# Identity transposes in TensorE's waits, and the first up products ahead of the second rows, in a two-layer streaming encoder

## Chip, cores and metric

One core of one Trainium2 chip. The metric is the device time of one execution in microseconds (us), the median of three runs.

## What is computed

Two layers of an encoder over 640 rows of 1024 numbers (512 of a prompt, 8 streams of 16 frames), all in fp32. Cut to what matters here, one layer is:

```
xn = rms_norm(x, norm1)
q|k|v|q_idx|k_idx|w_idx|u|v_s|g_a|g_b = xn @ w_in
att = sparse attention of q over the keys that the indexer selects
sg  = chunked spatial gating of u and v_s
h   = x + (sigmoid(g_a) * (att @ w_pa) + sigmoid(g_b) * (sg @ w_pb)) @ w_out
xf  = rms_norm(h, norm2)
g   = the best of 4 groups for a row (softmax of xf @ w_rg + b_rg)
e   = the best two of its 8 experts (softmax of xf @ w_re + b_re), weights that sum to 1
y   = h + sum over the two of weight * ((silu(xf @ w_eg[e]) * (xf @ w_eu[e])) @ w_ed[e])
```

After the second layer stands a last `rms_norm`. The new keys, values, index keys and gating rows are outputs too.

## The kernel before

Every engine has its own program, written out by hand, and the engines wait for each other on semaphores. TensorE's program (`pe`, from line 729) runs each layer in this order. `norm_transposes` (L734) turns a tile of 128 rows into `xt`: eight transposes by the identity per tile (L749), four to a bank, with banks 0 to 3 in turn. `proj_job` (L770) multiplies a tile by a block of `w_in` (L763). Attention, gating (L1045) and the output product (L1096) follow. While the output product runs, `route` (L1062) gives each finished tile's router logits.

Then comes the **dispatch**, the stretch in which rows are assigned to experts. VectorE picks each row's experts (`tile_route`), TensorE counts their ranks by products with a triangle of ones (`ranks`, L1069 and L1070), VectorE turns ranks into one-hot matrices (`place_front`, `place_back`, `dispatch`), and TensorE multiplies these into a table of rows (`table_rows`, L1076, and the product of L1121 for the rows beyond 64 of an expert). Between these steps TensorE waits for VectorE: `chosen_ready`, `onehot_ready` (2, 3 and 4), `need_ready`. With the table, GpSimd gathers rows from DRAM into `xin` (L687).

The **expert blocks** are 17 per layer, `NB`; each holds two experts with 64 rows each. For block b, `rows_step` waits for the gather and transposes the 128 rows by the identity (L1129); VectorE's `rows_out` copies them to `xin_t` with a gain (L1806), two copies of 512 columns per block; `up_step` multiplies by the two experts' gate and up weights (L1142, 32 instructions); ScalarE takes the silu (L1394); VectorE's `hidden_rows` multiplies (L1813); `across_step` transposes the hidden rows (L1148); `down_step` multiplies by the down weights (L1153); ScalarE copies out (L1403), and GpSimd scatters the result to `yd` (L692). TensorE's order is rows 0, rows 1, up 0, and then for each b: rows b+2, across b, up b+1, down b. `rows_step(b)` with b of 2 or more also waits for the copies of all blocks before b (`xin_ready`).

VectorE's order at the start of the blocks is fixed by its own program:

```
rows_out(0, 0)
rows_out(1, 1, 4)
pair_weights(L)
for b in range(NB):
    hidden_rows(b, b % XBUF, b % 2)
    if b + 2 < NB:
        rows_out(b + 2, b % 2)
```

`pair_weights` is `gates` (from L1484) and two instructions more (L1614, L1615); its result is used after the last block.

The weights of 12 experts fit at a time, in `places`. SyncE's program issues the loads of experts 12 and on in order: the gate and up weights of a pair when the up products of the block that holds their place are done (`gu_psum`, L416), then the down weights when that block's down products are done (`y_psum`, L426), and only then the next pair. Gathers and scatters go through GpSimd's own queue.

At the **boundary of the layers**, SyncE waits for the last scatters (`y_out`) and reloads each row's two results (L542); VectorE's `combine` adds them (L1833), and TensorE's `norm_transposes` for the next layer waits for each tile's sum (`x_new`).

Of the kernel before, what the change touches and what calls it, by code (L numbers as in the profile page):

```python
# [21 lines left out]
P = 128  # L22
# [39 lines left out]
NB = PLAIN + ALWAYS // 2  # L62
# [13 lines left out]
YBUF = 2  # L76
# [30 lines left out]
def filled(i, L, e):  # L107

    here = [v for v in LOADED if v % PLACES == i]
    return L * len(here) + len([v for v in here if v <= e])  # L110
# [18 lines left out]
def prior(name, L):  # L129

    return L * PER_LAYER[name]
# [25 lines left out]
def build(nc, a, o):  # L157
    ctx = ExitStack()
    with ctx:
# [3 lines left out]
        def sem(name):  # L163
            return ctx.enter_context(nc.semaphore(name))
# [116 lines left out]
        banks = [ctx.enter_context(nc.psum_tensor(f"bank{i}", [P, BLK], F32)) for i in range(8)]  # L281
# [47 lines left out]
        y_out = [sem(f"y_out{z}") for z in range(YBUF)]  # L329
# [31 lines left out]
        def gathers(q):  # L361

            return 16 * len(range(q, NB, XBUF))

        def scatters(z):

            return 16 * len(range(z, NB, YBUF))
# [362 lines left out]
        def _(pe):  # L730
            pe.wait_ge(s_ident, 1)
            idm = ident[:, :]

            def norm_transposes(phase, tiles, L):  # L734
                for t in tiles:
                    if phase:
                        pe.wait_ge(mt_done, prior("mt_done", L) + 2 * NT)
                        pe.wait_ge(xo_done, prior("xo_done", L) + 2 * t + 2)
                    elif L:
                        pe.wait_ge(x_new, prior("x_new", L - 1) + t + 1)  # L740
                    else:
                        pe.wait_ge(s_x[t], 16)
                    for hf in range(2):
                        n = 2 * t + hf
                        if n >= 4:
                            pe.wait_ge(xt_done, prior("xt_done", L) + 2 * NT * phase + n - 3)
                        for k in range(4):

                            mm = pe.transpose(banks[n % 4][:, k * P:(k + 1) * P],  # L749
                                              x[:, t, 4 * hf + k:D:KD], idm)  # L750
                        mm.then_inc(xt_psum, 1)

            for L in range(DEPTH):
# [16 lines left out]
                def proj_job(n):  # L770
                    u, t = PROJ_JOBS[n]
                    if t == 0:
                        wait_unit(u)
                    if u == KU:
                        if t + 1 < NT and (t or L):
                            norm_transposes(0, (t + 1,), L)
                        pe.wait_ge(xt_done, prior("xt_done", L) + 2 * t + 2)
                    if n >= 4:
                        pe.wait_ge(proj_free, prior("proj_free", L) + n - 3)
                    mm = project(u, t, banks[4 + n % 4][:, 0:width(u)], width(u))  # L780
                    mm.then_inc(proj_psum, 1)
                    if u == KU and t == 0 and not L:
                        norm_transposes(0, (1,), L)
                    if t == NT - 1 and u != IU:
                        pe.drain().then_inc(unit_done, 1)

                def fill(n):
# [10 lines left out]
                    if k1 == KD:  # L798
                        mm.then_inc(proj_psum, 1)
                        if t == NT - 1:  # L800
                            pe.drain().then_inc(unit_done, 1)

                norm_transposes(0, (0,), L)
                for n in range(2 * NT):
                    proj_job(n)

# [259 lines left out]
                def ranks(a, b):  # L1066
                    pe.wait_ge(chosen_ready, prior("chosen_ready", L) + b)
                    out = banks[RANK_BANK[a]][:, 0:EXPERTS * (b - a)]
                    pe.matmul(out, before, scr[:, P + EXPERTS * a:P + EXPERTS * b], start=True, stop=False)  # L1069
                    pe.matmul(out, ones, scr[:, P + EXPERTS * (NT + a):P + EXPERTS * (NT + b)],  # L1070
                              start=False, stop=True).then_inc(count_psum, 1)

                def table_rows(tiles):
                    for m in range(2 * tiles[0], 2 * tiles[-1] + 2):
                        for h in range(2):
                            mm = pe.matmul(banks[7][BR * h:BR * h + BR, 0:EXPERTS // 2], rank_hot[:, m, :],  # L1076
                                           place_hot[:, m, h:EXPERTS:2], start=(m == 0), stop=(m == 2 * NT - 1))
                    return mm

                for n in range(2 * NT):  # L1080
# [20 lines left out]
                    if t >= 1 and c == 0:  # L1101
# [4 lines left out]
                pe.wait_ge(onehot_ready, prior("onehot_ready", L) + 2)  # L1106
                pe.wait_ge(xo_done, prior("xo_done", L) + 2 * NT)
                table_rows(range(4))
                ranks(4, 5)

                pe.matmul(banks[6][0:EXPERTS, 0:1], earlier_tiles[:, NT - 1, :], ones[:, 0:1], start=True, stop=False)
                pe.matmul(banks[6][0:EXPERTS, 0:1], chosen[:, NT - 1, :], ones[:, 0:1], start=False, stop=True).then_inc(count_psum, 1)
                pe.wait_ge(onehot_ready, prior("onehot_ready", L) + 3)
                table_rows([4]).then_inc(table_psum, 1)
                pe.wait_ge(need_ready, prior("need_ready", L) + 1)
                pe.matmul(banks[6][:, P:P + EXPERTS + 1], need_rows, before[0:EXPERTS, 0:EXPERTS + 1],
                          start=True, stop=True).then_inc(start_psum, 1)
                pe.wait_ge(onehot_ready, prior("onehot_ready", L) + 4)
                for m in range(2 * NT):
                    for h in range(2):  # L1120
                        mm = pe.matmul(banks[7][BR * h:BR * h + BR, 256:256 + n_over // 2], rank_hot[:, m, :],  # L1121
                                       over_hots[:, m, h:n_over:2], start=(m == 0), stop=(m == 2 * NT - 1))
                mm.then_inc(table_psum, 1)
                pe.wait_ge(table_ready, prior("table_ready", L) + 1)

                def rows_in(b, q, first=0):

                    for k in range(KD):
                        mm = pe.transpose(banks[first + k // 4][:, (k % 4) * P:(k % 4 + 1) * P], xin[q][:, k:D:KD], idm)  # L1129
                    mm.then_inc(xin_psum[L], 1)  # L1130

                def up(two, z):
                    for k in range(KD):
                        for h in range(2):
                            if two[h] is places[SPLIT]:
                                for m in range(2):
                                    mm = pe.matmul(banks[2 + z][BR * h:BR * h + BR, P * m:P * m + P],
                                                   xin_t[z][:, k, BR * h:BR * h + BR], two[h][0][m][:, P * k:P * k + P],
                                                   start=(k == 0 and m == 0), stop=(k == KD - 1 and m == 1))
                                continue  # L1140
                            w = two[h][0].rearrange("p (m k f) -> p m k f", m=2, k=KD)
                            mm = pe.matmul(banks[2 + z][BR * h:BR * h + BR, 0:2 * P].rearrange("p (m f) -> p m f", m=2),  # L1142
                                           xin_t[z][:, k, BR * h:BR * h + BR], w[:, :, k, :],
                                           start=(k == 0), stop=(k == KD - 1))
                    mm.then_inc(gu_psum[L], 1)
# [12 lines left out]
                def two_of(b):  # L1158
                    return [places[(2 * b + h) % PLACES] for h in range(2)]

                def rows_step(b):
                    pe.wait_ge(x_in[b % XBUF], gathers(b % XBUF) * L + (16 * (b // XBUF) + 16))
                    if b >= 2:
                        pe.wait_ge(xin_ready[L], 2 * b)
                    rows_in(b, b % XBUF, 4 if b == 1 else 0)

                def up_step(b):
                    for h in range(2):
                        e = 2 * b + h
                        if b != OVER_AT:  # L1170
                            pe.wait_ge(up_in[e % PLACES], 32 * filled(e % PLACES, L, e))
                        else:
                            pe.wait_ge(more_up, 32 * ALWAYS * (L + 1))
                    pe.wait_ge(xin_ready[L], 2 * b + 2)
                    if b >= 2:
                        pe.wait_ge(h_done[L], b - 1)
                    up(two_of(b), b % 2)
# [17 lines left out]
                    down(two_of(b), b % 2)  # L1195

                rows_step(0)
                rows_step(1)
                up_step(0)
                for b in range(NB):  # L1200
                    if b + 2 < NB:
                        rows_step(b + 2)
# [696 lines left out]
```

## Time and profile before

| | |
|---|---|
| runs | 1440.35 us median of three, 1437.21 to 1441.36 |
| profiled execution | 1441.81 us, span 1440.0 us |
| TensorE matmul busy | 1315.8 us, 91% of the span, 5724 instructions |
| TensorE weight loads | 723.0 us, 50% |
| VectorE, ScalarE, GpSimd busy | 533.0 us, 339.7 us, 220.7 us |
| mean granted TensorE clock | 0.957 of full speed |
| HBM read, written | 199.44 MB, 27.78 MB |

Busy time is an average over stages with different limits. A granted clock of 1.00 is 2.4 GHz and one of 0.50 is 1.2 GHz; a stretch with both shows a number between. In the chain of waits, a row gives the time at which a piece of the chain starts, its length, and what it is: work of an engine at a line, a transfer, or "issue" where the profile shows nothing that was waited for. Some matmul records can be missing from a trace.

### The profile page before, as it was taken

To read this page: it belongs to the slowest core of one execution; us is meant where nothing else is said; L and a number is where in the kernel's file an instruction comes from. 1 tells how busy PE (TensorE), PEld (TensorE's weight loads), DVE (VectorE), ACT (ScalarE), POOL (GpSimd) and SP (SyncE) were. 2 spreads that over 40 slices of the span, in tenths; PEclk is the share of its full clock that TensorE was granted. 3 is DMA by queue.
4 is the path that set the end of the run, shared out by engine and by line. 5 is a ranking of instruction groups with operands and counts; after the bars stand their busy time and mean duration, and the time that the engine had idled before them with its cause. 6 is when DMAs were issued, how large, how long until landed. Compare 5 with 4: busy or idle time off the path is not lost.

```text
span 1440.0 us, 15437 instructions
## 1 busy us (share of the span) xinstructions
PE 1315.8 (91%) x5724; PEld 723.0 (50%) x5724; DVE 533.0 (37%) x1542; ACT 339.7 (24%) x773; POOL 220.7 (15%) x304
## 2 busy tenths in 40 slices
PE   7999999999999998998699999999999999979880
PEld 5654446544444555565385544464444445555550
DVE  1278895201110236321244779731011013462215
ACT  2132467200000101221213325651000010012221
POOL 6011024000000001233240200600000000022413
PEclk9989999999999997999799999999999999979995
DMA  8302102502402413999681111052060060379986
GB/s 241 117 13 60 59 1 72 175 0 66 153 0 95 183 73 134 372 409 402 260 207 59 51 33 49 8 145 95 0 219 0 0 263 30 117 273 404 405 314 242
DMA packets 96061, 208.77 MB, mean 145 GB/s; under 512 B 26529, under 2 KB 35969, under 8 KB 95985
## 3 DMA queue, kind: packets, MB, share of 16 engines
q1 hardware_dynamic: 81376, 181.27, 35.5%
q0 software_dynamic: 14608, 26.49, 5.3%
q8 instruction: 47, 0.77, 0.2%
q14 instruction: 30, 0.24, 0.0%
HBM read 199.44 MB, written 27.78 MB: 158 GB/s over the span
## 4 chain that ended last, share of the span: by engine, by line
PE 80%; DMA 5%; ACT 4%; issue 3%; DVE 3%; PEld 2%; PEldq 1%; SPq 0%; POOL 0%; POOLq 0%; ACTq 0%; DVEq 0%
PE bank L763 35%; PE bank L1045 10%; PE bank L1096 10%; PE bank L1142 7%; PE bank L796 3%; PE bank L1153 3%; DMA uv<-xd,mb 2%; PE bank L1129 2%; PE bank L845 1%; DMA more<-in_w_eu 1%; PE bank L1062 1%; PE bank L749 1%; PE bank L949 1%; PE bank L849 1%; PEldq L988 1%
## 5 line engine op out<-in xcount | busy, mean ns | idle before, releaser
L763 PE MATMUL bank<-ring,xt 128*128 128x512 f32 (+1 forms) x1120 | 433.9, 544 | 7.8 <-DMA ring<-in_w_in 5.0
L763 PEld LDWEIGHTS bank<-ring,xt 128*128 128x128 f32 x1120 | 213.8, 193 | 209.8 <-issue 190.2
L1766 DVE TENSOR_TENSOR scr<-scr,bank 128x512 f32<-128x512 f32 x20 | 13.7, 687 | 368.6 <-PE bank L1045 368.6
L1096 PE MATMUL bank<-ring,xt 128*128 128x512 f32 x320 | 141.3, 594 | 0.0
L557 POOL TENSOR_SCALAR stat<-stat 128x1 f32<-128x1 f32 (+1 forms) x27 | 10.4, 387 | 797.7 <-ACT uv L1229 614.1
L1373 ACT ACTIVATE scr<-bank,stat 128x512 f32<-128x512 f32 x40 | 25.3, 684 | 347.8 <-PE bank L763 347.8
L1096 PEld LDWEIGHTS bank<-ring,xt 128*128 128x128 f32 x320 | 59.3, 190 | 67.0 <-issue 67.0
L796 PE MATMUL bank<-ring,xt 128*128 128x512 f32 x160 | 76.7, 614 | 0.0
L1045 PE MATMUL bank<-ring,att 128*128 128x512 f32 x160 | 72.5, 596 | 2.2 <-ACT sgt L1365 1.8
L1045 PE MATMUL bank<-ring,sgt 128*128 128x512 f32 x160 | 71.9, 592 | 0.0
L763 PE MATMUL bank<-more,xt 128*128 128x512 f32 x160 | 70.3, 592 | 0.0
L1806 DVE TENSOR_TENSOR xt<-bank,gain 128x512 f32<-128x512 f32 x68 | 43.8, 685 | 66.4 <-PE bank L1129 66.4
L1142 PE MATMUL bank<-ring,xt 128*64 128x256 f32 x480 | 66.1, 382 | 1.5 <-issue 1.5
L1477 DVE MAX8 stat<-mb 128x8 f32<-128x256 f32 (+3 forms) x114 | 61.7, 541 | 3.0
L1477 DVE MATCH_REPLACE8 mb<-stat,mb 128x256 f32<-128x256 f32 (+3 forms) x114 | 59.7, 524 | 0.0
L692 POOL DMA_INDIRECT yd<-scr,mb x34 | 34.1, 1002 | 154.9 <-ACT scr L1403 149.7
L1813 DVE SCALAR_TENSOR_TENSOR xt<-bank,uv,xt 128x128 f32<-128x128 f32 x34 | 11.9, 351 | 116.5 <-ACT xt L1394 116.5
L1142 PE MATMUL bank<-qkv,xt 128*64 128x256 f32 x192 | 50.7, 424 | 3.2 <-issue 3.2
L1129 PEld LDWEIGHTS bank<-ident,uv 128*128 128x128 f32 x272 | 35.5, 197 | 31.9 <-issue 20.7
L1045 PEld LDWEIGHTS bank<-ring,att 128*128 128x128 f32 x160 | 29.9, 190 | 41.4 <-issue 39.1
L1142 PEld LDWEIGHTS bank<-ring,xt 128*64 128x64 f32 x480 | 39.2, 137 | 22.2 <-issue 4.3
L1777 DVE TENSOR_TENSOR x<-x,bank 128x512 f32<-128x512 f32 x20 | 13.8, 688 | 97.6 <-PE bank L1096 97.6
(288 smaller groups left out, 1806.1 us busy)
## 6 DMA issues: line engine op xcount, KB each, us to landing
ring<-in_w_in SPq DMA_DIRECT2D x12, 2048.0 KB, 9.4
ring<-in_w_ed SPq DMA_DIRECT2D x32, 512.0 KB, 17.8
ring<-in_w_eg SPq DMA_DIRECT2D x26, 512.0 KB, 11.1
ring<-in_w_eu SPq DMA_DIRECT2D x26, 512.0 KB, 17.5
ring<-in_w_out SPq DMA_DIRECT2D x4, 2048.0 KB, 12.9
qkv<-in_w_eg SPq DMA_DIRECT2D x12, 512.0 KB, 7.8
qkv<-in_w_eu SPq DMA_DIRECT2D x12, 512.0 KB, 10.1
more<-in_w_ed SPq DMA_DIRECT2D x12, 512.0 KB, 8.8
```

The lines of the kernel that those rows point to most:

```text
L692: pool.indirect_dma_start(out=yd, in_=yout[z], in_offset=None, out_offset=bass.IndirectOffsetOnAxis(ap=index(b, 1, q), axis=0), bounds_che ...
L749: mm = pe.transpose(banks[n % 4][:, k * P:(k + 1) * P], x[:, t, 4 * hf + k:D:KD], idm)
L763: mm = pe.matmul(out, xt[:, k, t * P:(t + 1) * P], rhs[:, k, :], start=(k == 0), stop=(k == KD - 1))
L796: mm = pe.matmul(banks[7][:, :], xt[:, k, t * P:(t + 1) * P], rhs[:, k, :], start=(k == 0), stop=(k == KD - 1))
L1045: mm = pe.matmul(b[2 + half_][:, :], src[:, j, t * P:(t + 1) * P], w[:, 4 * half_ + j, :], start=(j == 0), stop=(j == 3))
L1096: mm = pe.matmul(banks[5 + n % 3][:, :], xt[:, k, t * P:(t + 1) * P], w[:, k, :], start=(k == 0), stop=(k == KD - 1))
L1129: mm = pe.transpose(banks[first + k // 4][:, (k % 4) * P:(k % 4 + 1) * P], xin[q][:, k:D:KD], idm)
L1142: mm = pe.matmul(banks[2 + z][BR * h:BR * h + BR, 0:2 * P].rearrange("p (m f) -> p m f", m=2), xin_t[z][:, k, BR * h:BR * h + BR], w[:, :, ...
L1153: mm = pe.matmul(banks[4 + c][BR * h:BR * h + BR, :], hidden_t[z][:, BR * h:BR * h + BR], two[h][1][c] if two[h] is places[SPLIT] else two ...
L1373: ins = act.activation(scr[:, c0:c0 + 512], banks[4 * (n % 2) + m][:, :], ACT.Sigmoid, scale=rs1[:, n % NT:n % NT + 1])
L1477: make(*args, **kwargs).then_inc(dve_chain, 1)
L1806: V.tensor_tensor(xin_t[z][:, 4 * hf:4 * hf + 4, :], banks[first + hf][:, :].rearrange("p (k r) -> p k r", k=4), gain[:, L, 1, 4 * hf:4 * ...
```

## The change

TensorE gets a helper, `keep_busy(n, bank)`, that transposes the identity n times into the first 128 columns of a bank. Nothing reads the results. It is called

- at the start of layer 0: 8 times ahead of the first tile's transposes and 22 times behind them, bank 3;
- at the start of layer 1: 22 times ahead of the first tile's transposes, bank 3, behind a new wait for the last scatter of layer 0 (`y_out` of the last block's buffer);
- in each layer's dispatch, bank 1: 3 times ahead of `ranks(4, 5)`, 6 ahead of the last tile's `table_rows`, 9 ahead of the products of L1121, and 3 ahead of the wait for the table.

And `up_step(0)` now stands ahead of `rows_step(1)`. The other engines' programs are as before. The diff:

```diff
@@ -731,6 +731,11 @@
             pe.wait_ge(s_ident, 1)
             idm = ident[:, :]
 
+            def keep_busy(n, bank):
+
+                for _ in range(n):
+                    pe.transpose(banks[bank][:, 0:P], idm, idm)
+
             def norm_transposes(phase, tiles, L):
@@ -800,7 +805,12 @@
+                if L:
+                    pe.wait_ge(y_out[(NB - 1) % YBUF], scatters((NB - 1) % YBUF) * L)
+                keep_busy(22 if L else 8, 3)
                 norm_transposes(0, (0,), L)
+                if L == 0:
+                    keep_busy(22, 3)
                 for n in range(2 * NT):
                     proj_job(n)
@@ -1106,21 +1116,25 @@
                 table_rows(range(4))
+                keep_busy(3, 1)
                 ranks(4, 5)
 
                 pe.matmul(banks[6][0:EXPERTS, 0:1], earlier_tiles[:, NT - 1, :], ones[:, 0:1], start=True, stop=False)
                 pe.matmul(banks[6][0:EXPERTS, 0:1], chosen[:, NT - 1, :], ones[:, 0:1], start=False, stop=True).then_inc(count_psum, 1)
+                keep_busy(6, 1)
                 pe.wait_ge(onehot_ready, prior("onehot_ready", L) + 3)
                 table_rows([4]).then_inc(table_psum, 1)
                 pe.wait_ge(need_ready, prior("need_ready", L) + 1)
                 pe.matmul(banks[6][:, P:P + EXPERTS + 1], need_rows, before[0:EXPERTS, 0:EXPERTS + 1],
                           start=True, stop=True).then_inc(start_psum, 1)
+                keep_busy(9, 1)
                 pe.wait_ge(onehot_ready, prior("onehot_ready", L) + 4)
...
                 mm.then_inc(table_psum, 1)
+                keep_busy(3, 1)
                 pe.wait_ge(table_ready, prior("table_ready", L) + 1)
@@ -1195,8 +1209,8 @@
                 rows_step(0)
+                up_step(0)
                 rows_step(1)
-                up_step(0)
                 for b in range(NB):
```

Line numbers move: the identity transposes are L737, and L749 becomes L754, L763 L768, L1069 L1079, L1076 L1086, L1121 L1134, L1129 L1143, L1142 L1156, L1148 L1162.

TensorE at the start of layer 0, first before and then after (an x stands for that many products of the program in a row):

```order
L729 UNCONDITIONAL_BRANCH
L749 MATMUL bank<-ident,x 128x128 x8
L763 MATMUL bank<-ring,xt 128x276 x8
L749 MATMUL bank<-ident,x 128x128 x16
L763 MATMUL bank<-ring,xt 128x276 x8
```

```order
L729 UNCONDITIONAL_BRANCH
L737 MATMUL bank<-ident 128x128 x8
L754 MATMUL bank<-ident,x 128x128 x8
L737 MATMUL bank<-ident 128x128 x22
L768 MATMUL bank<-ring,xt 128x276 x8
```

Thirty transposes of the identity stand around those of the first rows, ahead of the first products with weights (L768).

TensorE in the dispatch of layer 0, from the ranks of the last tile to the first up products, first before and then after (`scr` holds the counts, `uv` the one-hot matrices and the gathered rows):

```order
L1069 MATMUL bank<-scr 128x32
L1070 MATMUL bank<-scr 128x32
L1111 MATMUL bank<-scr 32x1
L1112 MATMUL bank<-scr 32x1
L1076 MATMUL bank<-uv 64x16 x4
L1116 MATMUL bank<-scr 128x33
L1121 MATMUL bank<-uv 64x10 x20
L1129 MATMUL bank<-ident,uv 128x128 x16
L1142 MATMUL bank<-more,xt 64x256
L1142 MATMUL bank<-qkv,xt 64x256
```

```order
L737 MATMUL bank<-ident 128x128 x3
L1079 MATMUL bank<-scr 128x32
...
L737 MATMUL bank<-ident 128x128 x6
L1086 MATMUL bank<-uv 64x16 x4
L1128 MATMUL bank<-scr 128x33
L737 MATMUL bank<-ident 128x128 x9
L1134 MATMUL bank<-uv 64x10 x20
L737 MATMUL bank<-ident 128x128 x3
L1143 MATMUL bank<-ident,uv 128x128 x8
L1156 MATMUL bank<-more,xt 64x256
L1156 MATMUL bank<-qkv,xt 64x256
```

Before the up products there now stand eight transposes of gathered rows, those of block 0, instead of sixteen; the sixteen of blocks 1 and 2 follow behind them:

```order
L1156 MATMUL bank<-qkv,xt 64x256
L1143 MATMUL bank<-ident,uv 128x128 x16
L1162 MATMUL bank<-ident,xt 128x128
L1156 MATMUL bank<-qkv,xt 64x256
L1156 MATMUL bank<-sgt,xt 64x256
```

The transpose of the hidden rows of block 0 (L1162), which waits for VectorE, stands behind these sixteen, and the up products of block 1 behind that.

## Rows read from the trace of the kernel before

**Rows 1.** The page's slices: 40 of 36 us each, granted clock and transfers.
```profile
PEclk9989999999999997999799999999999999979995
GB/s 241 117 13 60 59 1 72 175 0 66 153 0 95 183 73 134 372 409 402 260 207 59 51 33 49 8 145 95 0 219 0 0 263 30 117 273 404 405 314 242
```

**Rows 2.** Timeline of TensorE at the start: start us, us, instruction [idle before, ended by].
```profile
4.51 1.95 PE L749 MATMUL bank<-ident,x 128*128 128x128 f32 x8 [4.51 <-DMA x<-in_x_prompt]
11.43 5.65 PE L763 MATMUL bank<-ring,xt 128*128 128x276 f32 x16 [4.97 <-DMA ring<-in_w_in]
...
18.90 3.99 PE L763 MATMUL bank<-ring,xt 128*128 128x276 f32 x16
```

**Rows 3.** Stretches around L1056: busy PE, PEld, DVE, ACT, POOL, then clock, transfers.
```profile
469.00:472.20 3.20, 1.02 (x10) 0.99 (x10) 2.58 (x10) 0.29 (x1) 0.00 (x0) 1.00 1.07 347
472.20:475.60 3.40, 3.40 (x18) 3.40 (x17) 0.00 (x0) 2.59 (x5) 0.00 (x0) 0.50 0.96 377
475.60:478.00 2.40, 2.40 (x19) 2.09 (x18) 0.00 (x0) 2.27 (x5) 0.00 (x0) 0.99 1.02 408
```

**Rows 4.** Timeline of TensorE in the dispatch of layer 0.
```profile
565.94 0.64 PE L1069 MATMUL bank<-scr 128*128 128x32 f32 x2 [0.92 <-DVE scr L1516]
...
569.10 0.61 PE L1076 MATMUL bank<-uv 128*64 128x16 f32 x8 [1.79 <-DVE uv L1555]
...
572.86 2.31 PE L1121 MATMUL bank<-uv 128*64 128x10 f32 x40 [2.58 <-DVE uv L1586]
575.95 1.94 PE L1129 MATMUL bank<-ident,uv 128*128 128x128 f32 x8 [0.78 <-DMA uv<-xd,mb]
```

**Rows 5.** Chain of waits, first expert blocks of layer 0: start us, us, what.
```profile
580.22 4.25 PE bank L1142 x32
...
586.32 0.36 DVE xt L1813
...
587.05 3.60 PE bank L1142 x32
...
593.56 3.60 PE bank L1142 x32
```

**Rows 6.** Timeline of VectorE around the pair weights of layer 0.
```profile
577.93 1.29 DVE L1806 TENSOR_TENSOR xt<-bank,gain 128x512 f32<-128x512 f32 x2 [0.75 <-PE bank L1129]
...
581.46 0.17 DVE L1484 TENSOR_REDUCE mb<-mb 128x5 f32<-128x20 f32 x1
...
583.94 0.49 DVE L1615 TENSOR_REDUCE mb<-scr 128x10 f32<-128x320 f32 x1
```

**Rows 7.** Timeline of SyncE's queue, loads of weights in layer 0.
```profile
585.81 0.45 SPq L416 DMA_DIRECT2D qkv<-in_w_eu  x1
592.41 0.33 SPq L426 DMA_DIRECT2D more<-in_w_ed  x1
```

**Rows 8.** Issue to landing, us: loads issued at 585.81, at 592.41, at 1286.21.
```profile
qkv<-in_w_eu SPq DMA_DIRECT2D x1, 512.0 KB, 9.8
more<-in_w_ed SPq DMA_DIRECT2D x1, 512.0 KB, 4.5
qkv<-in_w_eu SPq DMA_DIRECT2D x1, 512.0 KB, 10.5
```

**Rows 9.** Chain of waits, late expert blocks of layer 0 and the boundary.
```profile
641.67 18.68 DMA more<-in_w_eu
...
663.11 5.36 PE bank L1142 x32
...
704.23 3.17 DMA yd<-scr,mb
```

**Rows 10.** Timeline of TensorE at the boundary of the layers.
```profile
713.70 1.97 PE L749 MATMUL bank<-ident,x 128*128 128x128 f32 x8 [11.44 <-DVE x L1833]
716.94 1.94 PE L749 MATMUL bank<-ident,x 128*128 128x128 f32 x8 [1.27 <-DVE x L1833]
718.67 5.23 PE L763 MATMUL bank<-ring,xt 128*128 128x276 f32 x16
```

## The prediction

> **What bounds the kernel now.** I read the page first, its clock row and its transfer row [rows 1]; then TensorE's timeline at the places that the change touches [rows 2, 4, 10]; then the chain of waits through the first expert blocks [rows 5] and through the end of a layer [rows 9]. In [rows 1] the reader is to see two things. Each of the 40 digits of the clock row is a slice of 36 us: it stands at 9 nearly everywhere, and falls to 7 in the slice with the dispatch of layer 0 (the 16th), with the boundary of the layers (the 20th) and with the dispatch of layer 1 (the 36th). So the low clock is a matter of a few places, and the engine is near full clock otherwise. And in the slices of layer 0's expert blocks (the 17th to 19th) the transfers stand at 372 to 409 GB/s, about the highest of the run: there the weights arrive at the rate that the queue gives, and the chain waits for them, as in the 18.68 us of one load that ends it at 660.35 [rows 9]. What TensorE wins or loses in the first expert blocks must therefore get past the transfers before it reaches the end of the kernel.
>
> **The start: -1.7.** Eight transposes of the first rows took 1.95 us, 0.244 each, and the first eight products behind them 5.65 us; the next eight products took 3.99 [rows 2]. Only the clock differs between the two, so 5.65 - 3.99 = 1.66 us is what the low clock costs here. The change puts 8 transposes ahead of the first rows (8 x 0.244 = 1.95 us, before rows arrive at 4.51) and 22 behind them, from 6.46 on. At 0.244 they would end at 6.46 + 5.4 = 11.8, 0.4 us behind the weights that land for 11.43; at the price of the next paragraph's row (3.40 us for 18, 0.19 each) at 10.6, ahead of them. The ends are a loss of 0.4 and a gain of 1.66. I take the gain, since the nearest row shows such a run of transposes lifting the clock: in [rows 3] the engine did nothing but transposes from 472.2 to 475.6 at a granted clock of 0.50 (1.2 GHz), and the next stretch, transposes again, stands at 0.99 (2.4 GHz). What follows the start is TensorE's own work, so the gain stays.
>
> The Trainium skill states the contrary (TensorE: Matmul & The Clock Gate, Part 4: PE-mode transpose): the full clock does not engage for transposes, which do not count as activity of the engine in the same way. By that rule the sum would lose this gain and be 1.7 higher; by the row it keeps it. The rule comes back as a rival.
>
> **The boundary of the layers: -0.3.** The new wait ends when the last scatter has landed, 704.23 + 3.17 = 707.40 [rows 9]; the reloads behind it wait for the same event, so the wait itself costs nothing. 22 transposes then run to 711.6 (at 0.19) or 712.8 (at 0.244). The first rows' transposes start at 713.70, so nothing is delayed. But then the engine waits again: from 715.67 to 716.94 for the second rows [rows 10]. The upper end is the whole price of the low clock there: 1.94 - 1.05 for the second rows' transposes, where 1.05 is 8 at the 0.13 of [rows 3] (19 in 2.40 us), and 5.23 - 3.99 = 1.24 for the first products, together 2.1. The lower end is 0. I take -0.3, near the lower end, since between 469.0 and 472.2 a stretch with 1.02 us of transposes was enough for the clock to be at 0.50 behind it [rows 3], and from the end of the 22 until 716.94 there would be no more than one group of eight, which took 1.97.
>
> **The dispatch: 0.** Per layer 3 + 6 + 9 + 3 transposes go into four waits that TensorE has there anyway. At 0.244 they take 0.73, 1.46, 2.20 and 0.73 us, and the waits are 0.92, 1.79, 2.58 and 0.78 [rows 4]. All fit, the last by 0.05, so the cover is what VectorE and the gather do meanwhile; without it they would cost 5.1 us a layer. Do they lift the clock? Longest without a break are 9, half of what lies in the stretch of [rows 3] that lifted it, and between them stand products that are 10 or 16 columns wide. I take no gain; the upper end goes into the rival below.
>
> **The first up products ahead of the second rows: +1.5 and +0.7.** This is the part with a new wait, and what is queued behind it decides. Before, the second rows' transposes ended at 580.22 and the up products of block 0 followed [rows 5]. The copies for block 0 were done at 577.93 + 1.29 = 579.22 [rows 6], so they can now start at 579.25, 1.0 us earlier. But VectorE's order is unchanged: copy of block 0, copy of block 1, pair weights, then the hidden rows of block 0. The copy of block 1 waits for transposes that now stand behind the up products, and the pair weights, 581.46 to 583.94 + 0.49 = 584.43 or 2.97 us [rows 6], which ran beneath the up products, are now late behind it. From the end of the first up products to the second there were 2.6 us (584.47 to 587.05), with 0.73 from the hidden rows on (586.32 to 587.05) [rows 5]. Now there are 1.1 (eight transposes at 0.13) + 1.29 (copy) + 2.97 (pair weights) + 0.73 = 6.1, or 3.5 more.
>
> How much later the second up products start, S, has these ends. If the clock is full from 579.25 on, the first up takes the 3.60 of the second [rows 5], ends at 582.85, and S = 582.85 + 6.1 - 587.05 = 1.9. If it is low throughout, it takes twice that, 7.2, and S is 5.5. TensorE now idles from 577.89 to 579.25, where it used to transpose, so I expect the first up to run at the low clock for longer than before and to end at 584.5 to 585, which makes S about 3.8; and a hole of 6 us with 17 transposes in it is like the waits ahead of the up of 5.36 us at 663.11 [rows 9], which costs another 1.2 to 1.8. I take **S = 5**.
>
> What comes of S at the end? The next loads are issued behind block 0's down products, at 592.41 [rows 7], and would be issued at 597.4. The load before them was issued at 585.81 and landed 9.8 us later, at 595.6 [rows 7, 8]; the first of the next landed at 592.41 + 4.5 = 596.9, 1.3 us behind it. So the queue held 3.2 us of work at 592.41, and how much of this a later issue may use before the queue runs dry lies between 0 and 3.2; I take the middle, 1.6, which leaves a hole of 5 - 1.6 = 3.4 us. Against this, the gathers and scatters come later too: 128 rows of 1032 and of 1024 numbers, 1.05 MB, per block of 6.5 us (587.05 to 593.56 [rows 5]), at some 400 GB/s 2.6 us in 6.5, so 0.4 x 5 = 2.0 us less stands in the queue ahead of the late weights. The chain meets the transfers again at 663.11 with 3.4 - 2.0 = +1.4, say +1.5. In layer 1 the load in that place took 10.5 instead of 9.8 us [rows 8], so it has 0.7 more stock: +0.7.
>
> **The sum.** -1.7 - 0.3 + 0 + 1.5 + 0.7 = +0.2. The profiled execution took 1441.81 us; the sum makes it 1442.0. It is 1.5 above the median of 1440.35, and the runs shown spread by 4 us; against the median the forecast is 1440.35 + 0.2, **1440.5**. About 0.3%, 4.3 us, is what a measurement of this kernel can tell from no change.
>
> **The rivals.** *Slower: the queue runs dry.* The loads behind the first down products come S late and nothing makes it good: the full 5 us in each layer, less the 2.0 of the other parts, is +8.0, **1448.4**. It decides from an issue later than 592.41 + 3.2, which S = 5 exceeds. For it: the load at 592.41 landed close behind its forerunner. Against it: gathers and scatters come later by as much, and the chain waits 18.68 us for one load anyway [rows 9]. Chance 0.16.
>
> *Faster: the clock stays up.* The dispatch's transposes lift it before the first up products, and the boundary's hold it. Then S is 1.9, within the queue's 3.2, so the transfers lose nothing and have 0.4 x 1.9 = 0.8 less ahead of them in layer 0: -1.7 - 2.1 - 0.8 = -4.6, **1435.8**. For it: the run of transposes in [rows 3]. Against it: the waits between them. Chance 0.15.
>
> *Transposes do not hold the clock.* Then the added ones are idle time by another name: start and boundary give 0, the reordering stays, +2.2, **1442.6**. The trace speaks against it [rows 3]: 0.06. This is the rule of the Trainium skill's page (TensorE: Matmul & The Clock Gate, Part 4); the trace does not agree, with 0.99 behind 0.50 through transposes alone.
>
> **How the numbers follow.** The forecast has 0.63, the others 0.16, 0.15 and 0.06. The forecast's own bounds: S from 1.9 to 7, and a stock from 0 to 3.2, move each layer by some -0.8 to +4, the boundary -2.1 to 0; mostly that is 1436 to 1445. Taking in most of both rivals, I give 1435.0 to 1446.5. Faster by over 0.3% (under 1436.0): most of the second rival and a little of the forecast, 0.17. Slower (over 1444.7): the first rival and the forecast's upper edge, 0.20. Within: 0.63.
>
> **What would show it.** Right: the first eight products at 3.7 to 4.0 us instead of 5.65; the clock at 0.50 for most of the dispatch still; VectorE's pair weights behind the copy of block 1, and the second up products 4 to 6 us later against the first gather's landing; the loads behind the first down products as much later; the chain through a load at the late blocks again. Wrong: the first products still above 5 us (transposes do not count); the pair weights ahead of the copy of block 1; the clock full by the first up products; late blocks that wait 5 us longer than before in both layers.

## The result, and the profile after

The changed kernel takes **1454.31 us** (median of 6 runs, 1450.78 to 1456.42); the kernel before, beside it, 1440.86 (6 runs). The ratio is 1.0089, 95% interval 1.0068 to 1.0110: 13.4 us slower. The forecast was 1440.5, the range 1435.0 to 1446.5: wrong, and on the slow side. The profiled execution took 1453.69 us, its span 1451.9. In two of the experiments below one execution was a slow one (5552.48 us with the start's transposes alone, 1780.82 with two experts' weights early); it counts in the median given there and not in the ratio.

The page's slices, which answer to [rows 1]; a slice is now 36.3 us:

```profile
PEclk9989999999999997999899999999999999969995
GB/s 240 115 13 59 58 1 75 171 0 100 118 0 154 125 84 166 323 410 402 257 196 59 50 46 35 8 169 69 0 217 0 0 260 44 125 241 398 407 315 240
```

The clock digits hardly differ. Among the slices with dense transfers the first of the expert blocks of layer 0 stands out, the 17th: 323 GB/s, where [rows 1] had 372. There the time is looked for first.

TensorE's timeline at the start, which answers to [rows 2]:

```profile
4.69 1.97 PE L754 MATMUL bank<-ident,x 128*128 128x128 f32 x8 [1.02 <-DMA x<-in_x_prompt]
6.46 4.35 PE L737 MATMUL bank<-ident 128*128 128x128 f32 x22
11.62 3.99 PE L768 MATMUL bank<-ring,xt 128*128 128x276 f32 x16 [0.80 <-DMA ring<-in_w_in]
```

The first products take 3.99 us instead of 5.65; their weights landed 0.2 later. The start gains 1.5 us (the next group of products starts at 17.42 instead of 18.90), close to the forecast.

The chain of waits through the first expert blocks of layer 0, which answers to [rows 5]; L1156 are the up products (L1142 before), L1143 the transposes of gathered rows, L1820 the copies, L1827 the hidden rows:

```profile
574.73 1.96 PE bank L1143 x8
576.72 1.30 DVE xt L1820 x2
578.15 6.32 PE bank L1156 x32
584.47 1.10 PE bank L1143 x8
585.60 1.29 DVE xt L1820 x2
...
589.28 0.50 DVE mb L1629
589.80 0.36 DVE xt L1827
590.21 0.35 PE bank L1162
590.57 5.21 PE bank L1156 x32
595.78 1.75 PE bank L1167 x8
```

Three things are longer than in [rows 5]. The first up products take 6.32 us instead of 4.25. Between them and the second stand 590.57 - 584.47 = 6.10 us instead of 2.6: the copy of block 1 and all of the pair weights, the last of which ends at 589.28 + 0.50. And the second up products take 5.21 instead of 3.60. From the first rows' transposes to the first down products it is 595.78 - 574.73 = 21.05 us instead of 14.70 (575.95 [rows 4] to 587.05 + 3.60 [rows 5]): 6.35 us more.

SyncE's queue shows what hangs on that, and answers to [rows 7]: the last load behind the first up products, and the first behind the first down products.

```profile
586.57 0.43 SPq L416 DMA_DIRECT2D qkv<-in_w_eu  x1
597.54 0.33 SPq L426 DMA_DIRECT2D more<-in_w_ed  x1
```

It was 592.41; it is 597.54, though this execution came to the blocks 1.2 us earlier. The transfers from 586 to 606 us, 40 slices of 0.5 us, first before and then after:

```profile
GB/s 410 418 459 361 410 410 418 442 418 410 410 411 436 394 328 385 311 393 418 369 369 279 279 279 303 328 410 401 434 418 410 411 419 419 402 426 418 418 401 426
```

```profile
GB/s 401 410 410 369 393 369 377 385 393 418 418 426 254 157 198 141 0 0 0 0 0 0 0 0 0 213 295 434 393 401 328 221 270 287 295 377 369 360 401 418
```

Before, the rate never falls below 279. After, the queue is empty from 594 to 598.5, with thin slices on both sides. The dip before, from 596.5 to 598, is no sign of an empty queue: six loads had been issued from 592.41 to 595.59, and the last of them landed 10.4 us later, at 606.0; after the change a dip stands about as far behind the same loads, 221 to 295 from 601.5 to 603.5. From 592 to 604 the 24 slices have a mean of 376 GB/s before and 178 after: 2.4 MB less in 12 us, which at 410 GB/s is 5.8 us of transfers. The late end of layer 0 in the chain answers to [rows 9]:

```profile
668.10 5.36 PE bank L1156 x32
...
678.38 5.36 PE bank L1156 x32
...
709.40 3.17 DMA yd<-scr,mb
```

The up products that started at 663.11 start at 668.10, the last scatter at 709.40 instead of 704.23: 5.2 us later, 6.4 with the 1.2 us counted by which this execution came to the blocks earlier. Layer 1 repeats it; rows of the chain, first before and then after:

```profile
1276.15 3.65 PE bank L1129 x16
...
1286.70 3.60 PE bank L1142 x32
...
1406.58 3.24 DMA yd<-scr,mb
```

```profile
1281.53 1.96 PE bank L1143 x8
...
1284.94 6.21 PE bank L1156 x32
...
1297.36 5.09 PE bank L1156 x32
...
1418.55 3.24 DMA yd<-scr,mb
```

From the first rows' transposes to the first down products, 1302.45 - 1281.53 = 20.92 us instead of 1290.30 - 1276.15 = 14.15, or 6.77 more; the last scatter 11.97 later, of which 6.8 are new. So each layer ends as much later as its first down products come: from their start to the last scatter it is 113.58 us before (590.65 to 704.23) and 113.62 after (595.78 to 709.40) in layer 0, 116.28 and 116.10 in layer 1. The theory to test is therefore the first rival, **the queue runs dry**: the new order makes the first down products late, the loads behind them come late, and no part of that is made good. Against it stands a second theory, that the added transposes carry a part.

### The profile page after: what moved, and what is told of

Its sections match the earlier page's. It is cut to its first block, busy times and chain, and to the rows that moved or that the text cites. A ratio compares the mean times of both kernels' runs of the same rounds, so it can differ in the third digit from the quotient of the medians.

```text
span 1451.9 us, 15624 instructions
## 1 busy us (share of the span) xinstructions
PE 1341.3 (92%) x5818; PEld 743.2 (51%) x5818; DVE 533.1 (37%) x1542; ACT 339.5 (23%) x773; POOL 219.9 (15%) x304
## 4 chain that ended last, share of the span: by engine, by line
PE 80%; DMA 5%; ACT 4%; DVE 4%; issue 4%; PEld 2%; PEldq 1%; POOL 1%; SPq 0%; POOLq 0%; ACTq 0%; DVEq 0%
PE bank L768 34%; PE bank L1055 10%; PE bank L1106 10%; PE bank L1156 7%; DMA uv<-xd,mb 3%; PE bank L801 3%; PE bank L1167 3%; PE bank L1143 2%; PE bank L855 1%; PE bank L1072 1%; PE bank L754 1%; PE bank L959 1%; DVE x L1847 1%; PE bank L859 1%; PEldq L998 1%
## 5 line engine op out<-in xcount | busy, mean ns | idle before, releaser
L768 PE MATMUL bank<-ring,xt 128*128 128x512 f32 (+1 forms) x1120 | 432.8, 543 | 3.6 <-issue 1.8
L768 PEld LDWEIGHTS bank<-ring,xt 128*128 128x128 f32 x1120 | 213.0, 193 | 205.2 <-issue 190.4
L557 POOL TENSOR_SCALAR stat<-stat 128x1 f32<-128x1 f32 (+1 forms) x27 | 10.5, 389 | 798.7 <-ACT uv L1243 614.1
L1820 DVE TENSOR_TENSOR xt<-bank,gain 128x512 f32<-128x512 f32 x68 | 43.8, 686 | 80.9 <-PE bank L1143 80.9
L768 PE MATMUL bank<-more,xt 128*128 128x512 f32 x160 | 70.3, 592 | 0.0
L1156 PE MATMUL bank<-ring,xt 128*64 128x256 f32 x480 | 66.1, 382 | 1.2 <-issue 1.2
L1156 PE MATMUL bank<-qkv,xt 128*64 128x256 f32 x192 | 57.9, 469 | 3.5 <-issue 3.5
L1827 DVE SCALAR_TENSOR_TENSOR xt<-bank,uv,xt 128x128 f32<-128x128 f32 x34 | 11.9, 351 | 115.0 <-ACT xt L1408 114.9
L1143 PEld LDWEIGHTS bank<-ident,uv 128*128 128x128 f32 x272 | 34.1, 195 | 34.3 <-issue 23.0
L1156 PEld LDWEIGHTS bank<-ring,xt 128*64 128x64 f32 x480 | 39.2, 137 | 21.9 <-issue 4.0
L1055 PEld LDWEIGHTS bank<-ring,sgt 128*128 128x128 f32 x160 | 30.4, 190 | 38.3 <-issue 38.3
```

Of the source, the lines that this page charges most:

```text
L768: mm = pe.matmul(out, xt[:, k, t * P:(t + 1) * P], rhs[:, k, :], start=(k == 0), stop=(k == KD - 1))
L1055: mm = pe.matmul(b[2 + half_][:, :], src[:, j, t * P:(t + 1) * P], w[:, 4 * half_ + j, :], start=(j == 0), stop=(j == 3))
L1820: V.tensor_tensor(xin_t[z][:, 4 * hf:4 * hf + 4, :], banks[first + hf][:, :].rearrange("p (k r) -> p k r", k=4), gain[:, L, 1, 4 * hf:4 * ...
```

## The experiments

**1. The old order, all transposes kept.**

```diff
                 rows_step(0)
-                up_step(0)
                 rows_step(1)
+                up_step(0)
```

> The changed kernel with the second rows back ahead of the first up products; all identity transposes stay. Order theory (the loss of 13.4 us is the order alone: the second up products end 6.4 us later in each layer and nothing of it is made good): 1440.9 - 1.4 of the start = 1439.5, and the second up products of layer 0 near 585.7, 1.4 ahead of before. Transposes theory (the identity transposes in the dispatch and at the boundary carry a part of the loss, by delaying TensorE or shifting the clock): over 1441, up to the 1447 that half of the loss would give.

Measured: 1439.03 us, ratio 0.9982 (0.9969 to 0.9996). As the order theory had it; the second up products of layer 0 started at 582.18, earlier than the 585.7 given, mainly because this execution came to the blocks 3.6 us earlier than the kernel before. The chain shows one thing more, the first up products of both layers:

```profile
575.97 3.63 PE bank L1156 x32
```

```profile
1279.56 3.69 PE bank L1156 x32
```

They were 4.25 and 4.32 us: in the old order the dispatch's transposes can lift the clock ahead of them. They don't always: in the four kernels of experiments 8 to 11, with the same order and transposes, the same products took 3.69 us in four of eight cases and 4.21 to 4.67 in the others. Without the transposes, in five kernels of the old order, none took less than 4.16.

**2. The new order alone, on the kernel before**, without any transposes of the identity.

> The kernel before with the first up products ahead of the second rows and no identity transposes. Order theory: 1440.9 + 2 x 6.4 = 1453.7, between 1452.5 and 1455.5, the changed kernel's time with the start's 1.4 us given back. Transposes theory: 1447 to 1450, since half of the loss or more would be gone with the transposes.

Measured: 1452.93 us, 1.0093 (1.0068 to 1.0117). The order is the whole loss; the transposes theory falls.

**3. The pair weights ahead of the copy of block 1**, on the changed kernel (VectorE's program).

```diff
                 rows_out(0, 0)
-                rows_out(1, 1, 4)
                 pair_weights(L)
+                rows_out(1, 1, 4)
```

> The changed kernel with VectorE's pair weights ahead of the copy of block 1, so that they run beneath the first up products again. Queue theory (what counts is how late the second up products end): they start 2.1 us earlier, since the rows of block 2 still wait for that copy (586.9 + 1.2 + 0.3 = 588.4 instead of 590.5), and the shorter hole may spare 1.6 us of low clock, so 2.1 to 3.7 us less in each layer: 1454.3 - 4.2 to 7.4 = 1447 to 1450. If the loss had nothing to do with that delay (the new order hurts by the gathers or scatters it moves): no change, 1454. If there were stock for part of the delay (as I had predicted, 1.6 to 3.6 us of it), the loss would fall to 2 us a layer or less: under 1444.

Measured: 1443.75 us, 1.0025 (1.0008 to 1.0043); the profiled execution took 1447.49. The chain:

```profile
575.54 6.61 PE bank L1156 x32
...
586.03 3.60 PE bank L1156 x32
```

The hole is 586.03 - 582.15 = 3.9 us instead of 6.10, and the second up products are 1.6 us shorter: 3.8 us a layer, at the upper end of what I gave. The median lies 3 us below the range, and only the upper end of its interval (1447.6) and the profiled execution meet it; why the others are faster than the trace explains stays open. By the number alone the case with stock (under 1444) would be met; runs 4 and 5 speak against it.

**4. A delay of TensorE and nothing else**, on the kernel before, ahead of the up products of block 1; **5. the same delay six blocks later** (`b == 6`).

```diff
                     across_step(b)
+                    if b == 0:
+                        keep_busy(48, 6)
                     if b + 1 < NB:
                         up_step(b + 1)
```

> The kernel before, with 48 identity transposes between the transpose of the hidden rows of block 0 and the up products of block 1, in each layer: a delay at full clock and nothing else (48 x 0.11 = 5.3 us; no other order, VectorE as before). Queue-dry theory (the loads behind the first down products come 5.3 us later and nothing is made good): 1440.9 + 10.6 = 1451.5. Absorption as I had predicted it (a stock of 1.6 us and 0.4 of the delay, so 5.3 becomes 1.6 and 0.9): 1443.4. Clock theory (what hurts in the changed kernel is the low clock, and a delay with a busy TensorE costs little): under 1444.

> The kernel before, with the same 48 identity transposes six blocks later, ahead of the up products of block 7 (there a load takes 15 to 20 us from issue to landing, against 4.5 behind the first down products). Queue theory (a delay counts where the queue has nothing left and is hidden where loads stand in it): 1440.9, no more than 1442. If every delay of TensorE in the expert blocks reaches the end: 1451.5.

Measured: 1454.53 us, 1.0087 (1.0065 to 1.0110), and 1441.39 us, 1.0003 (0.9989 to 1.0018). The chain shows the same delay in both, at full clock, first ahead of block 1, then ahead of block 7:

```profile
587.45 5.24 PE bank L737 x48
592.69 3.60 PE bank L1147 x32
```

```profile
625.13 5.24 PE bank L737 x48
630.37 3.60 PE bank L1147 x32
```

This is the pair that decides. 5.24 us a layer, with no change of order, cost 13.4 us at one place (9.4 to 15.9 by the interval; 10.5 is the delay itself) and nothing at the other. In the profiled execution of the first, layer 1's first up products also took 5.70 us instead of 4.32, which nobody asked for (5.62 in the second). In the second, the 11th down products of layer 0 come 70.5 us behind the first instead of 65.6, and the 12th 78.1 instead of 77.8: TensorE's wait for the late loads takes the delay in. Behind the first the queue runs empty; its transfers from 586 to 606 us, in 0.5 us slices:

```profile
GB/s 410 401 442 361 401 410 393 401 410 451 426 410 386 427 320 189 90 49 25 8 0 0 0 0 0 0 180 377 377 410 434 320 107 172 246 320 320 287 320 426
```

Nothing was absorbed, and my stock of 1.6 us and credit of 0.4 of the delay (1443.4) are refuted.

**6. The low clock ahead of the first up products.** In experiment 3 these still took 6.61 us. On its kernel, six transposes go into the wait for the copy of block 0:

```diff
                 rows_step(0)
+                keep_busy(6, 5)
                 up_step(0)
                 rows_step(1)
```

> The kernel with the pair weights ahead (1443.8), and six identity transposes in the 1.47 us in which TensorE waits for the copy of block 0 ahead of the first up products (6 x 0.244 = 1.46, so they delay nothing). In all reordered runs so far the first up products ran at the low clock nearly throughout (5.2 to 6.6 us), in the old order with the same transposes they took 3.6 to 4.6. If that wait is what keeps the clock low: the first up takes 3.6 to 4.2, 2 to 2.7 us less in each layer, 1443.8 - 4 to 5.4 = 1438 to 1440. If the new order has too little work ahead of the first up products in any case (eight transposes of rows instead of sixteen): 1443.8, first up still over 5 us.

Measured: 1438.67 us, 0.9981 (0.9966 to 0.9995). The timeline of TensorE ahead of the up products, without the six and with them:

```profile
575.54 0.66 PE L1156 MATMUL bank<-more,xt 128*64 128x256 f32 x1 [1.47 <-DVE xt L1820]
```

```profile
574.60 1.48 PE L737 MATMUL bank<-ident 128*128 128x128 f32 x6
576.28 0.40 PE L1156 MATMUL bank<-more,xt 128*64 128x256 f32 x1 [0.19 <-DVE xt L1821]
```

Stretches of 4 us (busy PE, PEld, DVE, ACT, POOL, clock, transfers), again without and with; then the chain with them:

```profile
570.00:574.00 4.00, 4.00 (x37) 3.33 (x35) 2.95 (x13) 0.00 (x0) 2.10 (x3) 0.50 0.77 237
574.00:578.00 4.00, 2.53 (x13) 1.65 (x14) 3.62 (x15) 0.00 (x0) 0.00 (x0) 0.50 0.87 290
578.00:582.00 4.00, 4.00 (x22) 2.28 (x18) 0.28 (x1) 0.00 (x0) 0.00 (x0) 0.56 1.01 380
```

```profile
570.00:574.00 4.00, 4.00 (x49) 3.81 (x50) 3.56 (x16) 0.00 (x0) 2.97 (x3) 0.50 0.70 185
574.00:578.00 4.00, 3.81 (x26) 3.12 (x26) 3.15 (x14) 0.00 (x0) 0.01 (x1) 0.75 0.90 284
578.00:582.00 4.00, 3.04 (x27) 2.18 (x22) 1.82 (x4) 1.65 (x2) 0.00 (x0) 1.00 1.00 374
```

```profile
576.28 3.67 PE bank L1156 x32
```

Without the six TensorE stands still for 1.47 us while VectorE copies, and the granted clock stays at 0.50 (1.2 GHz) into the up products; with them it is at 1.00 (2.4 GHz) as they begin. The wait that the new order put ahead of the up products is what kept the clock low. Between 576.28 and 577 us it is 1.00, and layer 1's first up products take 3.67 as well. With both causes gone, the new order costs nothing against the old one (1439.03).

**7. The start's transposes alone**, on the kernel before.

> The kernel before with the 8 and 22 identity transposes at the start of layer 0 alone. If the start's gain stays to the end: 1440.9 - 1.4 = 1439.5, with first products of 4.0 us instead of 5.65 at 11.4. If transfers or a wait later in layer 0 take it back: 1440.9. If the transposes delay the first products: over 1441.3.

Measured: 1440.23 us, 0.9995 (0.9982 to 1.0009). Inconclusive: a gain of 1.5 us is within the interval, and so is none. That the first products are shorter is shown, above; that it reaches the end is not shown by this run alone.

**8 to 12. Filling the queue.** If the queue sets the end of a layer, earlier loads must pay where it is dry. Two edits of SyncE's program, on the kernel of experiment 1: expert 7's weights ahead of the wait for the second gather (`x_in[1]`), into a stretch with nothing to transfer; and the next pair's gate and up weights ahead of the last pair's down weights.

```diff
-                sp.wait_ge(x_in[1], gathers(1) * L + 16)
                 expert(7, EXPERTS * L + 7)
+                sp.wait_ge(x_in[1], gathers(1) * L + 16)
...
-                for e in range(PLACES, 2 * NB, 2):
+                for e in range(PLACES, 2 * NB + 2, 2):
...
-                    for v in units:
+                    for v in [v for v in (e - 2, e - 1) if v in LOADED and v >= PLACES]:
                         sp.wait_ge(y_psum[L], (v - PLACES) // 2 + 1)
                         expert_down(v % PLACES, EXPERTS * L + 2 * BLOCK_AT[v // 2] + v % 2, down_in[v % PLACES])
```

The first edit alone, then both, then the second alone:

> The first experiment's kernel (identity transposes, old order) with the weights of expert 7 issued ahead of SyncE's wait for the second gather, into the 4 us in which nothing is transferred (568 to 572 in layer 0): 1.5 MB or 3.7 us of transfers earlier. If the amount moved sets the end and the queue never runs dry later: 1439.0 - 2 x 3.7 = 1431.6. Queue-dry theory: the stock is only used up sooner; the loads behind the first down products are issued when they were, the queue is dry for 3 us more in front of them, and the gain is 0 to 1 us a layer: 1437 to 1439. If the load slows the first two gathers: up to 1443.

> As the one before, and SyncE issues the next pair's gate and up weights (due at that block's up products) ahead of the down weights of the pair before (due at its down products, 1.7 us later): the order in which TensorE frees the places and uses them. Queue-dry theory: 2 MB come 1.7 to 2.5 us earlier at the place where the queue is dry, so 1.5 to 3 us a layer less than the one before: 1432 to 1436. If the end is not set there: as the one before, 1437 to 1439, or more where down weights come late.

> The first experiment's kernel (1439.0) with the order of SyncE's loads alone changed: the next pair's gate and up weights ahead of the down weights of the pair before. If the two edits of the run before add up without helping each other: 1428.8 + 1.4 = 1430, nearly all of the gain from this one. If they need each other (an early load 7 pays only where the queue doesn't run dry behind it): the order alone fills a hole of 1 us a layer, 1435 to 1437, and the rest came with load 7.

Measured: 1437.59 (0.9970, 0.9955 to 0.9985), **1428.83** (0.9921, 0.9892 to 0.9951) and 1431.85 us (0.9939, 0.9918 to 0.9961). The transfers from 576 to 606 us, 40 slices of 0.75 us, with the first edit and with both:

```profile
GB/s 165 268 371 371 410 382 208 44 27 153 306 388 388 366 415 421 399 231 22 71 246 404 388 388 284 257 333 350 377 421 416 421 400 377 388 339 426 415 432 400
```

```profile
GB/s 311 273 322 322 235 317 361 306 240 180 300 393 404 406 378 410 399 421 399 361 355 404 399 432 416 416 421 394 404 426 421 399 421 433 400 416 421 393 426 426
```

The early load pays little by itself, since the queue then runs dry near 582 and near 590 instead; with the loads also issued as TensorE frees their places, it stays full from 584 on. What I had not expected is the size of the second edit: 1439.0 - 1431.9 = 7.2 us, where I had put the hole at 1 us a layer. It is not a filled queue: by 78 us behind the first down products of layer 0 the kernels with and without it had moved the same, 88.10 and 88.07 MB since the start. But the 12th down products come 73.9 us behind the first instead of 77.9 (78.1 instead of 82.2 in layer 1), and the last scatter of layer 0 109.7 instead of 113.9. So the gain is made in the late blocks, where the up products wait for gate and up weights [rows 9], which now come ahead of the down weights. That is read from the two traces; no run changes the order in the late blocks alone.

Two more stood beside these: expert 9's weights early too, and both edits on the kernel before, with no transposes.

> The kernel with both edits (1428.8), and expert 9's weights ahead of SyncE's wait for the second gather too, so 1.5 MB more before the expert blocks. If the queue has work to the end of the layer with it: up to 3.7 us a layer less, 1421.4. If the queue is dry in front of the first freed places instead: 1428 to 1429. If the first gathers, which all start from, now land behind these loads: 1 to 3 us a layer more, 1431 to 1435.

> The kernel before with the two edits of the loads and no identity transposes at all. If the transposes are worth what the first experiment showed (2.4 us) and stand beside the loads: 1428.8 + 2.4 = 1431. If they are worth more here, since every us ahead of the first up products is passed on: 1433.

Measured: 1436.34 (0.9960, 0.9944 to 0.9976) and 1432.72 us (0.9945, 0.9924 to 0.9966). The first is 7.5 us worse than with expert 7 alone, more than I gave for slower gathers. Its chain shows such a gather:

```profile
564.47 6.94 DMA uv<-xd,mb
```

In the changed kernel the first gather of the layer took 4.60 us. But the profiled execution was the fastest of that kernel, 1428.90, so where the rest of the loss lies stays open. The second differs from 1428.83 by 3.9 us in the medians, with overlapping intervals: whether the transposes are worth the 2.4 us of experiment 1 there is not shown.

## Why the prediction was wrong

**The start, -1.7: right**, -1.5 in the trace. The Trainium skill (TensorE: Matmul & The Clock Gate, Part 4: PE-mode transpose) has transposes not count for the full clock; the trace disagrees here too: 22 of them in 4.35 us, 0.20 each where eight ahead took 0.246 each, and products at 3.99 behind. Experiment 6 repeats it with six more transposes. At the start itself the low clock is read from durations alone: the granted clock of the profile reads 1.00 from 0 to 20 us in both kernels. And the last stretch of [rows 3] is not transposes alone, as the prediction says: two products of L1096 stand in it from 477.31 on. That the gain reaches the blocks no run shows: executions come to layer 0's first rows at 575.95 (before), 574.73 (after) and 573.21 us (experiment 2, without the start's transposes).

**The boundary, -0.3: nothing came of it.** The 22 transposes there end in time, and the clock is up behind them: 0.97 in the first rows' transposes, which take 1.16 us instead of 1.97. But it is at 0.50 again in the 1.46 us in which TensorE waits for the sums and in the second rows' transposes, which take 1.94 us again, and the first products take 5.64, no less than the 5.23 of [rows 10]:

```profile
719.00 1.16 PE L754 MATMUL bank<-ident,x 128*128 128x128 f32 x8 [1.80 <-DVE x L1847]
721.62 1.94 PE L754 MATMUL bank<-ident,x 128*128 128x128 f32 x8 [1.46 <-DVE x L1847]
723.36 5.64 PE L768 MATMUL bank<-ring,xt 128*128 128x276 f32 x16
```

From the last scatter of layer 0 to the first rows' transposes of layer 1 it is 572.13 us after (709.40 to 1281.53) and 571.92 before (704.23 to 1276.15).

**The dispatch, 0: right in this kernel**, whose first up products ran at the low clock all the same. In the old order the same transposes shortened them to 3.63 and 3.69 us in experiment 1 and in half of the cases behind it, so here it was the wait that the new order brings that made their worth nothing (experiment 6).

**The delay S = 5: right in kind, a little small.** The hole of 6.1 us was forecast from [rows 6] and measured as 6.10. The first up products came out at 6.32 us, where I had let them end at 584.5 to 585 from a start at 579.25, and the second at 1.6 us more, within the 1.2 to 1.8. S came out at 6.4, and at 6.8 in layer 1.

**What comes of S at the end, +1.5 and +0.7: this is the step that failed.** It was +6.4 and +6.8, the whole of S; with the 1.2 us by which this execution came to the blocks earlier and nothing from the boundary that makes +12.0, and the two profiled executions differ by 1453.69 - 1441.81 = 11.9. Both deductions were wrong:

- *The stock of 1.6 us.* I halved the 3.2 us between the issue at 592.41 and the landing of the load ahead of it [rows 8]. But that landing does not say how much is left to move. Experiment 4's kernel is the kernel before up to that issue, its loads 0.4 us later, and shows what the queue held: from 593 on its slices fall to 320, 189, 90, 49, 25 and 8 GB/s, 0.34 MB or 0.8 us at 410 GB/s, although the last load, issued at 586.20, lands 10.0 us later, at 596.2. And a load needs about 1 us from its issue to its first bytes: after the change, the issue at 597.54 is followed by transfers only from 598.5. So nothing was left that could take in a delay.
- *The 2.0 us of gathers and scatters that come later.* What comes later is transferred later, and still ahead of the layer's last weights. Time in which the queue is empty is lost; work that moves within the layer gives none of it back.

The totals bear both out: 12 us behind the start of layer 0's first down products the kernel before had moved 61.45 MB since its start, the changed kernel 61.59 and experiment 4's 61.41. Had the transfers gone on through a delay of 5 us, the later two would be some 2 MB ahead.

So the first rival was the mechanism (chance 0.16, 1448.4 us). It too was low, since it had S at 5: 1440.9 - 1.2 + 6.4 + 6.8 = 1452.9, 1.4 under the measured median. What I held against it, that the chain waits for loads later anyway, speaks for it: a chain that ends on transfers is one for which an empty queue is a loss. The other two rivals fall with their signs: the first up products ran at the low clock, 6.32 us, and the start's first products took 3.99 instead of staying above 5.

## What to carry over

Where transfers bound a stage, price a delay by the bytes that the queue still has to move at that moment, and not by when its last load lands: 5.24 us of TensorE's time in each of two layers cost over 9 us where the queue had about 0.8 us of transfers left, and nothing six blocks later. A delay put in for the purpose, as in experiment 4, shows in slices of half a microsecond what the queue held. And when a step is moved ahead on one engine, reorder the other engines that serve it: with VectorE's pair weights moved along and the new wait filled, the same order cost nothing. It gained nothing either; the gain came in the old order, where the loads were issued as places come free and one expert's load was moved early, 1428.83 us.

## What the runs showed of the hardware

- With TensorE still for 1.47 us ahead of the up products the granted clock stayed at 0.50 into them (6.61 us for 32 products); with six transposes in that wait it was 1.00 and they took 3.67.
- An empty queue takes about 1 us from the issue of a load to moving bytes: issued at 597.54, zeros up to 598.5; in experiment 4 issued at 598.05, zeros up to 599.
- A queue can be nearly idle well before its last load lands: in experiment 4 the transfers were under 200 GB/s from 593.5 on, and the last load landed at 596.2.
